# Gathering tokens for two experts at a time, and the last norm inside the expert stage

## What is computed

```
def moe_ffn(h, router, w1, w3, w2):
    logits = (h @ router).astype(jnp.float32)
    top_val, top_idx = lax.top_k(logits, TOP_K)
    top_w = jax.nn.softmax(top_val, axis=-1)
    gate = jnp.sum(jax.nn.one_hot(top_idx, N_EXPERTS, dtype=jnp.float32) * top_w[..., None], axis=-2)
    out = gate[..., 0:1].astype(h.dtype) * swiglu(h, w1[0], w3[0], w2[0])
    for e in range(1, N_EXPERTS):
        out = out + gate[..., e:e + 1].astype(h.dtype) * swiglu(h, w1[e], w3[e], w2[e])
    return out
...
        h = layer_norm(DEEPNORM_ALPHA * h + f, ln2_g[l], ln2_b[l])
```

## Time and profile before

| what | value |
|---|---|
| time, median of 3 runs | 1962.6 us (1962.38 to 1964.43) |
| the profiled execution | 1963.32 us, its span 1961.5 us |
| PE, DVE, ACT busy | 97%, 73%, 58% of the span |
| mean granted TensorE clock | 0.991 of full |
| the expert stage with its prologue, and the end | 895 to 1961.5 us |
| first up unit of expert 0 | 922.30 us |
| one expert, from one to the next | 127.8 us |
| last down matmul of expert 7 | 1935.95 us |
| HBM read | 452 MB, 232 GB/s over the span; some 338 GB/s in the expert stage |

### The profile page before, as it was taken

How to read it: one execution, slowest core, us unless ns; L and a number is a source line. 1 busy time by engine, 2 the same in 40 slices (tenths; PEclk the granted TensorE clock), 3 DMA queues, 4 the chain that set the end, 5 groups by cost and what they waited for, 6 DMA issues and landing times. The chain is left out here.

```text
span 1961.5 us, 27193 instructions
## 1 busy us (share of the span) xinstructions
PE 1910.4 (97%) x11117; PEld 1649.6 (84%) x11117; DVE 1423.7 (73%) x1600; ACT 1134.7 (58%) x1256; POOL 90.0 (5%) x156
## 2 busy tenths in 40 slices
PE   6999999999999999999999999999999999999995
PEld 5889999999977889998888888888888888888884
DVE  4876265644338763575988979879799798897996
ACT  2465343544334663435776767767677677676773
POOL 5002000100031020001000000000000000000000
PEclk9999999999999999998999999999999999999998
DMA  6232174554421332462999999989999999999992
GB/s 170 86 94 93 44 199 134 172 169 156 153 77 45 93 114 65 104 230 65 372 357 318 370 327 350 370 300 373 344 334 368 318 358 357 317 373 331 343 369 106
DMA packets 260485, 456.98 MB, mean 233 GB/s; under 512 B 32218, under 2 KB 111274, under 8 KB 260356
## 3 DMA queue, kind: packets, MB, share of 16 engines
q1 hardware_dynamic: 258966, 454.74, 67.7%
q10 hardware_dynamic: 1390, 0.44, 0.1%
HBM read 452.11 MB, written 3.04 MB: 232 GB/s over the span
## 5 line engine op out<-in xcount | busy, mean ns | idle before, releaser
L390 DVE TENSOR_TENSOR wl<-ring,wh 128x2048 fp32r<-128x2048 f32 x385 | 880.5, 2289 | 245.3 <-ACT wh L384 242.1
L384 ACT ACTIVATE wh<-ring 128x2048 fp32r<-128x2048 f32 x385 | 739.6, 1923 | 318.0 <-PE ps L359 317.9
L359 PE MATMUL ps<-wh,xgh 128*128 128x512 f32 x896 | 354.3, 395 | 2.4 <-DVE wl L390 2.4
L359 PE MATMUL ps<-wh,xgl 128*128 128x512 f32 x896 | 349.3, 390 | 0.0
L359 PE MATMUL ps<-wl,xgh 128*128 128x512 f32 x896 | 349.1, 390 | 0.0
L359 PE MATMUL ps<-hPh,ringr 128*128 128x288 f32 x1024 | 229.3, 305 | 0.0
L359 PEld LDWEIGHTS ps<-wh,xgh 128*128 128x128 f32 x896 | 168.3, 188 | 40.0 <-DVE wl L390 5.7
L359 PEld LDWEIGHTS ps<-wh,xgl 128*128 128x128 f32 x896 | 168.2, 188 | 35.8
L359 PEld LDWEIGHTS ps<-wl,xgh 128*128 128x128 f32 x896 | 168.4, 188 | 33.2
L359 PEld LDWEIGHTS ps<-hPh,ringr 128*128 128x128 f32 x1024 | 170.6, 189 | 6.2 <-issue 2.5
L359 PE MATMUL ps<-hPl,ringr 128*128 128x288 f32 x512 | 152.0, 297 | 0.0
(11 more groups left out here) (415 smaller groups left out, 2792.2 us busy)
## 6 DMA issues: line engine op xcount, KB each, us to landing
ring<-in_moe_w SPq DMA_DIRECT2D x336, 1024.0 KB, 5.4
ring<-in_w_in SPq DMA_DIRECT2D x38, 1024.0 KB, 5.2
ring<-in_ffn_w SPq DMA_DIRECT2D x33, 1024.0 KB, 5.2
ring<-in_w_out SPq DMA_DIRECT2D x8, 1024.0 KB, 10.0
ring<-in_w_in SPq DMA_DIRECT2D x32, 128.0 KB, 3.2
ring<-in_w_oa SPq DMA_DIRECT2D x16, 256.0 KB, 5.3
ring<-in_w_ob SPq DMA_DIRECT2D x8, 512.0 KB, 7.2
resid<-in_x_prompt SPq DMA_DIRECT2D x1, 1024.0 KB, 5.2
```

The costliest lines, as they stand in the source:

```text
L359: ins = nc.tensor.matmul(*a, **k)
L384: nc.scalar.activation(wh[:, k % WS, :], ring[:, s:s + SLOT], ACT.Copy).then_inc(hi_ready, 1)
L390: ins = nc.vector.tensor_tensor(wl[:, k % WS, :], ring[:, s:s + SLOT], wh[:, k % WS, :].bitcast(F32), ALU.subtract)
```

## The change

- `xgh` and `xgl` hold two experts (a dimension of 2); `xgl` moves over constants that are dead by then. `oh` is 256 columns wide.
- `gather` works on 256 columns, for two experts. The prologue gathers experts 0 and 1; experts 1, 3 and 5 gather the next pair (k 0 to 3 behind down units 2 to 5, k 4 to 7 behind units 8 to 11); experts 0, 2, 4, 6 gather nothing. Half of the channels now fills all four banks, so k = 4 waits until ACT has emptied them.
- `gathered` makes two copies per call, at u = 34, 35, 40, 41 of experts 1, 3, 5. Unit 0 of every expert waits for both halves of its pair's tokens.
- `y_ready` comes for each half of the columns, and `scatter` waits for each.
- The last norm stands in the expert block: statistics of a token tile behind its `scatter_add`, gain and bias loaded over `htokl` behind the last weight load, a first Sqrt on ACT behind `hidden_out`, the flag read before expert 7's `hidden_out`/`hidden_rest`. PE does one `idle_products` before the last scatter.

```diff
@@ up_unit
-                    if g == 0 and q < 2:
-                        pe.wait_ge(xg_ready, 2 * i + q + 1)
+                    if u == 0:
+                        pe.wait_ge(xg_ready, 2 * (i // 2) + 2 if isinstance(i, int) else 2 * i - NE + 2)
...
@@ down_units
-                        if ahead and 2 <= j < 2 + KD:
+                        if ahead and (2 <= j < 6 or 8 <= j < 12):
                             if j == 2:
-                                pe.wait_ge(oh_ready, i + 2)
-                            gather(pe, j - 2, htokh, 0)
-                            gather(pe, j - 2, htokl, 2)
-                        if j == 2 + KD:
+                                pe.wait_ge(oh_ready, (i + 1) // 2 + 1)
+                            if j == 8:
+                                pe.wait_ge(xg_ready, i + 2)
+                            gather(pe, j - 2 if j < 6 else j - 4, 2 * CAP)
+                        if j == 7:
                             turn_slots(pe, i)
...
@@ gather
-                def gather(pe, k, h, b):
-                    for t in range(NT):
-                        ins = rel.mm(ps[b + k // 4][:, CAP * (k % 4):CAP * (k % 4) + CAP], h[:, t, P * k:P * k + P],
-                                     oh[:, t, :], start=(t == 0), stop=(t == NT - 1))
+                def gather(pe, k, w):
+                    for h, b in ((htokh, 0), (htokl, 2)):
+                        for t in range(NT):
+                            ins = rel.mm(ps[b + k % 4 // 2][:, 2 * CAP * (k % 2):2 * CAP * (k % 2) + w], h[:, t, P * k:P * k + P],
+                                         oh[:, t, 0:w], start=(t == 0), stop=(t == NT - 1))
                     if k % 4 == 3:
                         ins.then_inc(ga_done, 1)
...
@@ expert_scalar, gathered
-                    if on and u in (34, 35, 38, 39):
-                        gathered(act, i + 1, (u - 34) // 4, u % 2)
+                    if on and i % 2 and u in (34, 35, 40, 41):
+                        gathered(act, (i + 1) // 2, (u - 34) // 6, u % 2, 2 * CAP)
...
+                def gathered(act, p, h, low, w):
+                    act.wait_ge(ga_done, 2 * p + h + 1)
+                    for z in range(2):
+                        k, e = 4 * h + 2 * z, w // CAP
+                        v = ps[2 * low + z][:, :].rearrange("p (k e t) -> p k e t", k=2, e=2)[:, :, 0:e, :]
+                        ins = nc.scalar.activation((xgh, xgl)[low][:, 0:e, k:k + 2, :].rearrange("p e k t -> p k e t"), v, ACT.Copy)
+                    if low:
+                        ins.then_inc(xg_ready, 1)
...
@@ the expert block, SP
                     for e in range(1, NE):
+                        if e == NE - 1:
+                            more = crowded(sp)
                         expert_loads(sp, e, e, 0)
-                    more_rounds(sp, lambda i, e: expert_loads(sp, i, e, 0))
+                    sp.wait_ge(ga_done, NE)
+                    more_rounds(sp, more, lambda i, e: expert_loads(sp, i, e, 0), lambda: sp.wait_ge(ga_done, NE + 2 * NE * (ROUNDS - 1)))
+                    sp.dma_start(gb[:, 0, :], A["ln2_g"][1].partition_broadcast(P)).then_inc(gb_in, 16)
+                    sp.dma_start(gb[:, 1, :], A["ln2_b"][1].partition_broadcast(P)).then_inc(gb_in, 16)
...
@@ the expert block, PE
                     for k in range(KD):
-                        if k % 4 == 0:
-                            pe.wait_ge(tok_ready, 1 + k // 4)
-                        gather(pe, k, htokh, 0)
-                        gather(pe, k, htokl, 2)
+                        if k in (0, 2):
+                            pe.wait_ge(tok_ready, 1 + k // 2)
+                        if k == 4:
+                            pe.wait_ge(xg_ready, 1)
+                        gather(pe, k, 2 * CAP)
...
+                        if not on:
+                            pe.wait_ge(ohT_ready, NE)
+                            idle_products(1)
                         scatter(pe, e, 0)
...
@@ the expert block, DVE
-                    onehot(0)
+                    onehot(0, 1)
                     low_half(1)
...
-                            if u == 5 and e < NE - 1:
-                                dve.wait_ge(ga_done, 4 * e + 4)
-                                onehot(e + 1)
+                            if u == 5 and e % 2 and e < NE - 1:
+                                dve.wait_ge(ga_done, e + 1)
+                                onehot(e + 1, e + 2)
...
                     for t in range(NT):
                         scatter_add(dve, NE - 1, t)
+                        dve.wait_ge(sc_added, 1 + NT * (NE - 1) + t + 1)
+                        tile_stats(s, t)
...
+                    more_rounds(dve, more, again, stats_again)
+                    V.tensor_scalar(rstd[:], mv[:, :, 1], LN_EPS, None, ALU.add).then_inc(var_ready, 1)
+                    dve.wait_ge(gb_in, 32)
```

More of the change, by code:

```diff
@@ L100, in program @@
         ones = sb("ones", [P, P])
+        with ExitStack() as mem:
+            xgl = mem.enter_context(nc.sbuf_tensor("xgl", [P, 2, KD, CAP], F32R))
         cumU = sb("cumU", [P, P])
@@ L584, in masks, with tile_stats, tile_moments, norm @@
             keep(c, "pool")
-        gb_in, tail_zero = sem("gb_in"), sem("tail_zero")
+        gb_in, tail_zero, late_step = sem("gb_in"), sem("tail_zero"), sem("late_step")
         var_ready, std_ready, hat_ready = sem("var_ready"), sem("std_ready"), sem("hat_ready")
         nrm_turned, out_stored = sem("nrm_turned"), sem("out_stored")
-        def norm(call, j, g_vec=None, b_vec=None, final=False):
-            gb = gb_all
+        def tile_stats(c, i):
+            n = TILES[i][1]
+            for a in range(2):
+                c(nc.vector.bn_stats(stats[0:n, i, a, :], resid[0:n, i, 512 * a:512 * a + 512]))
+        def tile_moments(c, i):
+            n = TILES[i][1]
+            c(nc.vector.bn_aggr(mv[0:n, i, :], stats[0:n, i, :, :].rearrange("p a b -> p (a b)")))
+        def norm(j):
             with nc.Block() as block:
@@ L596, in _ @@
                 def _(sp):
[L597 to L607 removed]
+                    load_units(sp, 0, 3)
                 @block.vector
@@ L643, in _ @@
                 def _(act):
-                    act.wait_ge(var_ready, call + 1)
+                    act.wait_ge(var_ready, 1)
                     nc.scalar.activation(std[:], rstd[:], ACT.Sqrt).then_inc(std_ready, 1)
-                    for k in range(0, 0 if final else KD, 2):
+                    for k in range(0, KD, 2):
                         act.wait_ge(nrm_turned, k + 1)
@@ L652, in _ @@
                 def _(pe):
-                    idle_products(0 if final else 0)
-                    for k in range(0 if final else KD):
+                    for k in range(KD):
                         for i, (t0, n) in enumerate(TILES):
@@ L2562, in more_rounds @@
                                 body(r * NE + e, e)
+                        if after:
+                            after()
                 @block.gpsimd
@@ L2619, in _ @@
                         up_units(pe, e, 3 if e else 0)
-                        down_units(pe, e, on)
+                        down_units(pe, e, on and e % 2)
                         if on:
@@ L2638, in again @@
                             scatter(pe, i, t)
-                    more_rounds(pe, again)
+                    more_rounds(pe, crowded(pe), again)
                 @block.scalar
@@ L2674, in again @@
                         hidden_out(act, i)
-                    more_rounds(act, again)
+                    more_rounds(act, more, again)
+                    act.wait_ge(var_ready, 2)
+                    nc.scalar.activation(std[:], rstd[:], ACT.Sqrt).then_inc(std_ready, 1)
                 @block.vector
@@ L2766, in again, with stats_again @@
                             scatter_add(dve, i, t)
-                    more_rounds(dve, again)
-        norm(0, 0)
+                    def stats_again():
+                        late = Chain(dve, late_step)
+                        dve.wait_ge(sc_added, 1 + NT * NE * ROUNDS)
+                        for t in range(NT):
+                            tile_stats(late, t)
+                        late.sync()
+                        for t in range(NT):
+                            tile_moments(late, t)
+                        late.sync()
+                    more_rounds(dve, more, again, stats_again)
+                    V.tensor_scalar(rstd[:], mv[:, :, 1], LN_EPS, None, ALU.add).then_inc(var_ready, 1)
+                    dve.wait_ge(gb_in, 32)
+                    for i, (t0, n) in enumerate(TILES):
+                        s(V.scalar_tensor_tensor(out=resid[0:n, i, :], in0=resid[0:n, i, :], scalar=mv[0:n, i, 0:1],
+                                                 in1=gb[0:n, 0, :], op0=ALU.subtract, op1=ALU.mult))
+                    dve.wait_ge(std_ready, 2)
+                    s.link(V.reciprocal(rstd[:], std[:]))
+                    for i, (t0, n) in enumerate(TILES):
```

(5 more changed lines are left out.)

123 lines of the change are left out of this document (56 added, 67 removed).

## The result

The changed kernel takes 1948.44 us (median of four runs, 1947.70 to 1948.71), the kernel before 1963.51 us in the same comparison. The ratio is 0.9922, with a 95% interval of 0.9905 to 0.994. The forecast was 1949.5 us. It was reckoned down from a median of 1962.6 us; in this comparison the kernel before took 0.9 us more, so the drop is 15.1 us where 13.1 were forecast.

The account below looks back on a forecast made before the run. The prediction took PE to bound the expert stage. Its terms, -21.8 + 1.8 + 1.7 + 6.55 + 1.7 - 3.05 = -13.1 us, gave 1949.5 us, a factor of 0.993, range 1944.5 to 1956.5.

Parts of the forecast that it names:

- prologue: First gather before unit 0 of expert 0: more one-hots and ACT's uncovered copies delay unit 0 to 928.85, +6.55 us.
- half clock: Prologue: two PE idles of over 2 us bring one stretch at 1.2 GHz, +1.7 us (0 to 3.4).
- gathers: Expert stage: 24 wide pieces at 0.77 us replace 56 narrow at 0.72, gain 21.8 us (20.6 to 23).
- hand-over: Behind experts 1, 3, 5: unit 0 waits for ACT's last copies, 0.6 us three times, +1.8 us (0 to 3.5).
- one-hots: Experts 1, 3, 5 after unit 5: six instead of three make PE wait 0.59 us each, +1.7 us (0 to 2).
- end: After the last down matmul: norm statistics done at 1947.9 instead of 1950.66, no row wait, gain 3.05 us (2 to 3.7).
- Rival 1: Expert stage: transfers bind, so the gathers' 21.8 us don't come, 1971.3 us, chance 6%; milder ceiling at 358 GB/s, 1953.5, 5%.
- the gap of 1.69 us: Ahead of the last norm's statistics in the kernel before: said to hold flag read, jump and block edge.
- What would show it: Signs in the trace: experts at 122 and 129 us, splits 2.72 us apart, `xgl` releases, landings within 10 us, end 22.5.
- Rival 2: Prologue and hand-overs cost their upper bounds: copies in pieces at 1.5 times, two half-clock stretches, 1954.7 us, chance 14%.
- Rival 3: PE has uncounted slack: no one-hot term, no clock stretch, jump free, 1945.5 us, chance 15%.
- Rival 4: At the end the norm gains nothing, as jump and flag reads take what the block edge took: 1951.5 us, chance 8%.

Follow-up runs that it names:

- e11: The changed kernel run once more, unaltered: 1947.88 us, ratio 0.9927 to the kernel before.
- e4: The changed kernel with products of the identity filling PE's two waits in the prologue: 1947.19 us, ratio 0.9912 to the kernel before.
- e10: The kernel of e9 with the later one-hots of e6 and the earlier gathers and copies of e7: 1938.52 us, ratio 0.9875 to the kernel before.
- e7: The changed kernel with wide gathers one down unit earlier and ACT's copies one unit earlier: 1946.38 us, ratio 0.9913 to the kernel before.
- e6: The changed kernel with the six one-hots of experts 1, 3 and 5 after unit 17 instead of 5: 1947.01 us, ratio 0.9919 to the kernel before.
- e1: The kernel before with only the last norm moved into the expert stage, gathers left one expert at a time: 1958.58 us, ratio 0.9975.
- e8: The changed kernel without the loop for crowded experts, no branch or flag read on all four engines: 1947.98 us, ratio 0.9921 to the kernel before.
- e5: The changed kernel without gathers, copies and one-hots of experts 1, 3, 5 and without the crowded-expert loop: 1926.77 us, ratio 0.9812 to the kernel before.
- e2: The changed kernel with its last norm put back into a block of its own: 1952.21 us, ratio 0.9944 to the kernel before.
- e3: The changed kernel with the second half of the first gather written to free PSUM banks 4 to 7: 1943.69 us, ratio 0.9897 to the kernel before.
- e9: The kernel of e3 with DVE instead of ACT copying the low parts in the prologue: 1941.0 us, ratio 0.989 to the kernel before.

## Why the prediction was right, point by point

The sum of the spans' difference, term by term. The forecast's columns are those of its sum:

| term | forecast | measured | from |
|---|---|---|---|
| ahead of the stage | 0 | -0.8 | 894.21 against 894.98; not the change's (e11) |
| prologue | +6.55 | +5.97 | 33.29 against 27.32 us |
| half clock | +1.7 | +1.64 | period of expert 0, changed against e4 |
| gathers | -21.8 | -22.4 | seven periods before (891.96) against e10 (869.53) |
| hand-over | +1.8 | +2.2 | changed against e7 |
| one-hots | +1.7 | +1.7 | changed against e6 |
| end | -3.05 | -3.3 | 22.26 against 25.55 us |
| rest | | -0.2 | what the last rows don't cover of -15.2 |
| sum | -13.1 | -15.2 | |

**The number.** 1949.5 us stands against 1948.44, but the sum of terms missed by 2.1 us, as the table shows, and the kernel before ran 0.9 us above the median that the forecast started from. That brought the two numbers closer, by luck. The forecast put the part ahead of the stage at nothing; it moves by up to 3 us from trace to trace (893.25 in e1, 896.27 in e8), which is more than the terms for the hand-over, the one-hots or the clock.

**What bounds the kernel.** Right. PE bounds every expert, and where its wait went something on PE was next. Rival 1 was the one case on the other side, and e5 excludes it in the strongest way: a stage without any gather runs at 122.1 us an expert.

**Gathers.** The step's size was a little off, the price of a wide k. I took 0.77 us, by adding to six wide matmuls the 0.05 us that six narrow ones leave over. From the periods of e10 a gather of eight wide pieces costs 127.93 - 122.11 = 5.82 us, 0.73 a k. A narrow one was 127.82 - 122.11 = 5.71, 0.71 a k. So 256 columns cost hardly more than 128, and the rest of 0.05 us did not carry over. In the stage that is 24 x 0.04 = 1 us more gain, of which 0.3 is lost again because a narrow k was 0.71 and not 0.72.

**Prologue.** Every step of it came, with the release by ACT's `xgl` named ahead. From the first gather to unit 0 I had 11.35 us, measured are 10.87, of which 8 x 0.05 = 0.4 us is the same price of a k. The first gather is 0.48 us later than before, counted from the stage's start; I had 0.62.

**Clock.** One stretch at half clock, 1.64 us, against 1.7. The forecast took one because it lies between none and two, and that one came in this trace is luck: e2 and e8 had two, and paid 1.4 to 1.5 us more. The bounds of 0 to 3.4 were the right ones.

**Hand-over and one-hots.** The waits stand at the places named: 0.33 us on PE at 1177.46, 1428.73 and 1679.97, and 0.36 us at 1080.04, 1331.30 and 1582.54. At the hand-over unit 0 starts 0.48 us late (1177.46 against 1176.98, which is 0.45 behind the last pair), and the restart of the array adds 0.11: the 0.6 us of the forecast. What e7 takes away is 0.72 us each time, so the term was 0.4 us too small over three. The one-hots cost 0.57 us a time, as forecast. With both waits gone a period with a gather falls by 1.1 us, from 129.05 to 127.9 (e10).

**End.** 22.3 us against a forecast of 22.5. The jump cost 0.65 us where I took 0.6, and e8 shows that it is the jump. What the prediction said of the gap of 1.69 us was misread, though: DVE's flag read was over (1944.3) before DVE fell idle at 1944.75, and 1.0 us of the gap was the wait for PE's jump of 3.75 us. The gain came out right because the changed kernel has nothing left that waits for PE. No run takes PE's jump alone out of the kernel before, so that this would be worth about 1.0 us there is an estimate from 1946.1 less 1945.0. PE also does its last scatters at full clock now, with 0.80 us of standstill where 2.31 us brought the clock down; no run separates that from the statistics between DVE's adds. The Trainium skill ("Runtime: NRT & Kernel Launch", Instruction fetch mechanics) names such a wait for a taken branch. The trace agrees that there is one, of 0.65 us on DVE and 3.6 on PE, but no run shows that it is the fetch.

**What would show it.** Experts of 122 and 129 us, unit 0 of experts 2, 4 and 6 released by `xgl`, 22.3 us at the end for 22.5: all seen. Loads landed in 5.7 us in the median and 8.8 at most. Two signs were put too narrowly. The splits of expert 0's down units are 2.72 us apart except at two places, 3.19 and 3.77 us, where PE also turns hidden values and slots; and units of expert 2 come up to 4.53 us apart behind its start, but they do so in the kernel before as well. Rival 2 did not come: pieces of 128 make ACT's copies no dearer (590 ns for one, before 574). Rival 3 did not either, since each wait showed. Rival 4 falls with e1, where the norm alone takes 3.24 us off the end; its price of 1951.5 us doesn't follow from the sum either, which without the term of 3.05 is 1952.6. Of the 15.2 us between the two traces 0.8 belongs to the run and not to the change.

## What to carry to other kernels

Where a small stationary operand is multiplied by few columns, count instructions, not columns: two experts' tokens in one gather cost PE 0.73 us a k, one expert's 0.71. Batching like this pays wherever PE bounds the loop, but it needs a second buffer or spare banks at its edges, or the copies that were hidden stand alone. Here they took back 5.97 us of 22, and 1.64 more by the clock, at the one place where nothing else ran. That was avoidable: free banks, an idle engine for half of the copies, and one-hots and copies moved to where nobody waits for them brought another 9.4 us.

A wait of two microseconds on the matrix engine costs more than itself when the clock falls behind it; dummy products in the wait are a cheap cure, and removing the wait a better one.

At a block edge, look for the engine that arrives last, even when it has no work left. Here it was PE, with a jump of 3.75 us, and the engine on the critical path stood beside it.

## What the runs showed of the hardware

- PE standing still for 2.15 us was followed by 3 to 4 us at a granted clock of 0.50, not each time, and once or twice in programs that are the same at that place. With the wait filled to 0.43 us it did not happen (e4), nor without the waits (e3, e9, e10). At the end of the kernel before the same followed 2.31 us of standstill, in the changed kernel nothing followed 0.80 us.
- A jump over a loop that isn't taken costs DVE 0.65 us when nothing hides it (the changed kernel and e1; without it none, e8). PE's queue is at the same jump for 3.4 to 3.9 us in all eleven traces that have it, which is hidden unless another engine waits for PE.
- fp32r matmuls of 256 columns start 0.12 us apart in the gathers (three in 0.36 us in the prologue, six in 0.71 in the stage), those of 128 columns 0.112 (48 in the 5.38 us before unit 0, kernel before).
- One core moves 361 GB/s over 840 us, nearly all of it read from HBM, without a loss to PE (e5).
- The part of the program ahead of this stage differs by up to 3 us from trace to trace with nothing changed in its work: its end was read at 893.25 to 896.27 us.
